# Where the SBUF tiles of a three-layer model kernel begin: tables in front, large tiles on multiples of 256 bytes

## The reference, cut to what matters

```python
q = (hc @ w_query).reshape(PEER_CHUNK, PEER_HEADS, PEER_KEY_DIM)
# top 16 of 128 keys for each half, top 16 of their 256 sums: experts, gate
u = jnp.take(expert_u, experts, axis=0)
act = jax.nn.gelu(jnp.einsum('chkd,cd->chk', u, hc))
v = jnp.take(expert_v, experts, axis=0)
return jnp.einsum('chk,chkd->cd', gate * act, v)
```

## Time and profile before

| | us |
|---|---|
| median of three runs | 3251.67 |
| the profiled execution | 3249.77 |
| its span, first to last instruction | 3247.7 |
| PE busy | 3108.9 |
| POOL busy | 1771.1 |
| DVE busy | 1605.6 |
| ACT busy | 1151.8 |

### The profile page before, as it was taken

One profiled execution on the slowest core, in us unless ns is written; L12 is line 12 of the kernel. 1 busy time (PEld: TensorE's weight loads), 2 busy tenths in 40 slices (PEclk: granted clock), 3 DMA queues, 4 the chain that ended last, 5 costly groups with the idle time before them and its releaser, 6 DMA issues.

```text
span 3247.7 us, 44125 instructions
## 1 busy us (share of the span) xinstructions
PE 3108.9 (96%) x14602; PEld 2502.0 (77%) x14602; DVE 1605.6 (49%) x2785; ACT 1151.8 (35%) x1478; POOL 1771.1 (55%) x2040
## 2 busy tenths in 40 slices
PE   5988999999999999997999999999999999999998
PEld 3777788876578887775788888888888788888886
DVE  7873454322435551694407996444411444444443
ACT  4354322236332213433323325555543322232222
POOL 3833677645047766573455665444446665566663
PEclk8989999999999999998999999999999999999999
DMA  7511455423025553221233444555564655555652
GB/s 304 207 36 61 151 186 191 153 71 96 1 78 200 187 187 112 87 88 61 85 98 112 146 136 169 184 184 184 188 240 141 217 200 186 179 169 196 202 191 72
DMA packets 170201, 481.94 MB, mean 148 GB/s; under 512 B 15360, under 2 KB 48896, under 8 KB 168080
## 3 DMA queue, kind: packets, MB, share of 16 engines
q1 hardware_dynamic: 147680, 410.83, 38.8%
q10 hardware_dynamic: 22448, 70.14, 5.6%
HBM read 411.70 MB, written 69.21 MB: 148 GB/s over the span
## 4 chain that ended last, share of the span: by engine, by line
PE 56%; issue 21%; POOL 19%; DVE 2%; ACT 1%; DMA 0%; DVEq 0%; POOLq 0%; SPq 0%; ACTq 0%
PE ps L1623 52%; POOL w_lo L548 19%; PE pa L1623 3%; DVE s_acc L1417 1%; DMA e_g<-expert_act 0%; DVEq L1414 0%; DVE s_pb L1429 0%; DVE s_tmp L1468 0%; DVE mg_lo L1470 0%; ACT mg_hi L918 0%; DVE s_m L1466 0%; DVE x L1122 0%; ACT L614 0%; POOLq L546 0%; POOLq L552 0%
## 5 line engine op out<-in xcount | busy, mean ns | idle before, releaser
L548 POOL TENSOR_TENSOR w_lo<-raw,w_hi 128x256 fp32r<-128x256 f32 x2036 | 1770.9, 902 | 1446.4 <-ACT w_hi L566 1444.5
L1623 PE MATMUL ps<-h_hi,w_hi 128*128 128x512 f32 x2392 | 950.2, 397 | 43.2 <-POOL w_lo L548 19.6
L1623 PE MATMUL ps<-h_hi,w_lo 128*128 128x512 f32 x2392 | 939.7, 393 | 0.0
L1623 PE MATMUL ps<-h_lo,w_hi 128*128 128x512 f32 x2392 | 915.7, 390 | 0.0
L566 ACT ACTIVATE w_hi<-raw 128x1024 fp32r<-128x1024 f32 x509 | 538.8, 1060 | 844.4 <-PE ps L1623 727.9
L1623 PEld LDWEIGHTS ps<-h_hi,w_hi 128*128 128x128 f32 x2392 | 454.9, 190 | 145.2 <-issue 25.9
L1623 PEld LDWEIGHTS ps<-h_hi,w_lo 128*128 128x128 f32 x2392 | 454.6, 190 | 95.3
L1623 PEld LDWEIGHTS ps<-h_lo,w_hi 128*128 128x128 f32 x2392 | 450.3, 188 | 93.3 <-issue 1.7
L1623 PE MATMUL ps<-wa_hi,w_lo 128*128 128x512 f32 x1024 | 408.6, 399 | 0.0
L1623 PE MATMUL ps<-wa_lo,w_hi 128*128 128x512 f32 x1024 | 403.5, 394 | 0.0
L1623 PE MATMUL ps<-wa_hi,w_hi 128*128 128x512 f32 x1024 | 401.5, 392 | 0.3 <-DVE x L1587 0.3
(11 more groups left out here) (315 smaller groups left out, 3088.7 us busy)
## 6 DMA issues: line engine op xcount, KB each, us to landing
ada<-in_ada SPq DMA_DIRECT2D x144, 512.0 KB, 4.4
raw<-in_expert_u SPq DMA_DIRECT2D x128, 512.0 KB, 4.1
raw<-in_expert_v SPq DMA_DIRECT2D x128, 512.0 KB, 4.2
raw<-in_ffn_in SPq DMA_DIRECT2D x88, 512.0 KB, 3.5
expert_act<-g_act ACTq DMA_DIRECT2D x128, 256.0 KB, 4.3
gate_matrix<-w_st ACTq DMA_DIRECT2D x16, 2048.0 KB, 6.7
e_w<-gate_matrix SPq DMA_DIRECT2D x16, 2048.0 KB, 11.2
e_g<-expert_act SPq DMA_DIRECT2D x128, 256.0 KB, 7.8
```

The lines of the kernel that those rows point to most:

```text
L548: last = nc.gpsimd.tensor_tensor(w_lo[:, k, c:c + 256], raw[:, k, c:c + 256], w_hi[:, k, c:c + 256].bitcast(F32), ALU.subtract)
L1623: return nc.tensor.matmul(out, a, b, start=start, stop=stop_)
```

## The change

The small tables move to the front, behind them `big` is rounded up so that `base + big` is a multiple of 256, and all large tiles, rstd, ada, cvec, keys and the arena follow in their old order at that phase (ada4's 16 bytes now lie in front, AR is no longer rounded). `mg_hi` and `mg_lo`, which were placed at h's old offsets by number, follow `h_off`. `r_z` leaves the arena's end, which is 32 bytes shorter, for the unused part of rstd. No instruction, wait or DMA is added or removed.

```diff
@@ -161,13 +161,7 @@
     K = 1024
-    x = at("x", 0, [DT, S])
-    h_hi = at("h_hi", 16 * K, [DT, S], F32R)
-    h_lo = at("h_lo", 32 * K, [DT, S], F32R)
-    raw = at("raw", 48 * K, [RING, 1024])
-    w_hi = at("w_hi", 64 * K, [RING, 1024], F32R)
-    w_lo = at("w_lo", 80 * K, [RING, 1024], F32R)
-    misc = 96 * K
+    misc = 0
     cols = at("cols", misc, [COLS["end"]])
     misc += 4 * ((COLS["end"] + 7) // 8 * 8)
     mod = at("mod", misc, [144])
@@ -175,6 +169,16 @@
     misc += 768
     consts = at("consts", misc, [CONST["end"]])
     misc += 4 * ((CONST["end"] + 7) // 8 * 8)
+    ada4 = at("ada4", misc, [RING])
+    big = (base + misc + 16 + 255) // 256 * 256 - base
+    x = at("x", big, [DT, S])
+    h_off = big + 16 * K
+    h_hi = at("h_hi", h_off, [DT, S], F32R)
+    h_lo = at("h_lo", big + 32 * K, [DT, S], F32R)
+    raw = at("raw", big + 48 * K, [RING, 1024])
+    w_hi = at("w_hi", big + 64 * K, [RING, 1024], F32R)
+    w_lo = at("w_lo", big + 80 * K, [RING, 1024], F32R)
+    misc = big + 96 * K
     rstd_off = misc
     rstd = at("rstd", misc, [S])
     misc += 2 * K
@@ -187,9 +191,7 @@
     keys = at("keys", misc, [2, NK])
     misc += 1 * K
-    ada4 = at("ada4", misc, [RING])
-    misc += 32
-    AR = (misc + 31) // 32 * 32
+    AR = misc
     arena_bytes = 229344 - base - AR
@@ -267,8 +269,8 @@
-    mg_hi = at("mg_hi", 16 * K, [DT, S], F32R)
-    mg_lo = at("mg_lo", 32 * K, [DT, S], F32R)
+    mg_hi = at("mg_hi", h_off, [DT, S], F32R)
+    mg_lo = at("mg_lo", h_off + 16 * K, [DT, S], F32R)
@@ -292,7 +294,7 @@
-    r_z = ar("r_z", 92 * K, [2, TT, PH])
+    r_z = at("r_z", rstd_off + 64, [2, TT, PH])
```

## The result

The changed kernel took 3228.76 us (median of four, 3223.73 to 3236.50) against 3251.81 for the kernel before (median of four): a ratio of 0.9924 with a 95% interval of 0.9905 to 0.9943. In a second group of runs the same kernel gave 3229.91 against 3249.81, 0.9940 (0.9920 to 0.9961). The change makes the kernel 20 to 23 us faster; 3223 were forecast.

The account below looks back on a forecast made before the run. The prediction took one PE matmul stream to bound nearly everything after 280 us; terms for wa, f, cy, pm and c summed to 29.1 us, taking 3249.77 to 3220.7, or 3223 us as the runs' median. The range was 3205 to 3256.

Parts of the forecast that it names:

- The wa term: Stage streaming wa_hi and wa_lo: 3072 matmuls each 6.6 ns faster, 20.3 us saved.
- The pm and cy terms: Matmuls on pm and cy: 96 each, faster by 5.0 and 6.6 ns, saving 0.5 and 0.6 us.
- c, 0.7: Matmuls on c, 204 with pm's phases: 1.0 us by count, 0.7 taken because the 48 turned ones have less to give.
- The h term: The 7176 matmuls on h, in phase before and after: 0 taken, bounds 97 us gain and 47 us loss.
- The f term: Two FFN output stages streaming f_hi and f_lo: 1056 matmuls each 6.6 ns faster, 7.0 us saved.
- Is it all on the path?: Check in the wa and f stretches that other engines stay under PE's faster pace, POOL next; nothing taken off.
- the sum: All off-phase streams (wa, f, cy, pm, c) going to 226.8 ns a matmul: 29.1 us saved in total.
- The rival of a further gain from a start at 0: A start at 0 speeds the h stream too: 47 us more (3175 us), or 138 on all streams (3084 us); 7%.
- The rival on the other side: The h stream loses its good remainder 128 and pays 6.6 ns a matmul: 47 us added, 3270 us; 6%.
- The rule of 16-byte lines: Skill's SBUF rule: full speed wants two or more hits per 16-byte line; by it alone no stream would gain, sum 0.
- the 111 us on top: Extra gain if alignment alone kept all streams from the skill's 216 ns: 10.8 ns on each of 10248 matmuls.
- the 138 us: Extra gain if all streams reached the 213.3 ns of their columns: 13.5 ns on each of 10248 matmuls, 3084 us.

Follow-up runs that it names:

- e8: Changed kernel with the 12 ada blocks of the FFN output stages issued beside the first 8 weight blocks, not 5: 3224.79 us, ratio to before 0.9921.
- e5: Changed kernel with the weights (raw, w_hi, w_lo) at 192 modulo 256 and everything else at 64, 128 bytes apart: 3280.65 us, ratio to before 1.0088.
- e4: Changed kernel with only the weights (raw, w_hi, w_lo) moved, to 224 modulo 256, the rest at 0: 3284.79 us, ratio to before 1.0098.
- e1: Changed kernel with only the arena 32 bytes later, at 32 modulo 256: 3254.01 us, ratio to before 0.9992.
- e3: Changed kernel with all large tiles and the arena 32 bytes later, all at 32 modulo 256: 3232.22 us, ratio to before 0.9934.
- e7: Changed kernel run again unedited, for its spread and a second profile: 3229.91 us over six runs, ratio to before 0.9940.
- e9: Changed kernel with the weights at 0 modulo 512 and the other large tiles at 256 modulo 512, 256 bytes apart: 3231.24 us, ratio to before 0.9930.
- e6: Changed kernel with the weights (raw, w_hi, w_lo) at 192 modulo 256 and everything else at 0, 64 bytes apart: 3244.39 us, ratio to before 0.9985.
- e2: Changed kernel with only the arena 64 bytes later, at 64 modulo 256: 3231.67 us, ratio to before 0.9937.

## Why the prediction was right

The wa term was 20.3 us: the stage went from 717.55 to 697.50, 20.1 less. The pm and cy terms, 0.5 and 0.6: 22.46 to 21.92 and 22.57 to 21.92, 0.5 and 0.7. c, 0.7: the stage went from 54.56 to 53.94, 0.6. Moving the tables and r_z cost nothing that the traces show, and neither did the new remainder on ACT, DVE and POOL. The h term, taken as 0 between -97 and +47 us, measured 0.0 on the two pieces of the chain; only the longest h stretch (2064 matmuls, router work between them) took 564.82 and 564.81 us in the two profiles, against 563.05 before and 563.69 in e8. What that up to 1.8 us is stays open.

The f term was mis-sized. 7.0 us were forecast; the first profile shows 1.3 + 0.3, the second 2.6 + 2.2, where 3.5 + 4.4 is what the stages give without stops. The step that failed is "Is it all on the path?": it compared the engines' busy times over the middle of an f stage and named POOL as next. What was next is at the stage's start, on SP's queue: ada blocks, each behind a wait for DVE, ahead of weight blocks. The earlier trace rows hides this, since the stretch begins 31 us into the stage; the waits of the stage in the kernel before (us, times, longest) show it:

```profile
ACT w_hi L566 <- DMA raw<-in_ffn_out: 23.2, 3, 12.9
```

The late blocks were there already, and PE at 233 ns was just slow enough to meet them hardly at all (0.9 us in both stages together). The rest of the difference between 29 and 20 to 23 us goes with the clock, as far as the runs show it: beside e5 to e8 the kernel before ranges over 17 us, and in the three groups its runs lose some 2.6 to 3 us for each 0.001 of mean granted clock. Six runs of the changed kernel had a mean of 0.978 beside 0.9805 for the kernel before; two of the first four, at 0.980 and 0.981, took 3223.7 and 3223.9. Whether the short stops of the f stages pull the clock down is not settled: in the first profile it fell to the lower level 1 us after the stop that ends at 1227.91, and e8, which has no such stops, had 0.9797. Over all kernels the mean is 0.981 to 0.982 in e4 and e5, whose streams are all slow, 0.980 in e1 and the kernel before, and 0.978 in e3, e7 and e9. So the clock may give back part of what a faster stream wins; no run separates the two.

The clearest check of the sum is e8's profile beside that of the kernel before, since TensorE was at its lower level about as long in both (127 and 130 us) and neither waits long in an f stage: 3220.04 against 3249.77 us, 29.7 less, where the sum had 29.1 and the edit to the order is worth 0.9 in the old layout. That the changed kernel itself came out within 7 us of 3223 is the mechanism, less what the stops and the clock took; neither of these was a term of the forecast.

The reasoning had the right rule among several, and for this change the number couldn't tell them apart. "Same phase on both sides" and "multiple of 64 or 256" all gave 227 here; e3 separates them, e4 to e6 show the other side, and the title's 256 turned out to be sufficient and not needed. The rival of a further gain from a start at 0 is out with e3 and e9: 227.0 ns is the pace at each common remainder tried (128, 0 and 32). The rival on the other side, that 128 is a good remainder by itself, is out too. Its price of 6.6 ns on the h stream was of the right size: e4 made that stream pay 6.4 ns, and the kernel lost 33 us against before, with a mean granted clock of 0.982 against 0.980. The 10248 matmuls with which the prediction and the expectations price "all streams" are h and wa alone; with all 12084 the 111 us on top would be 131 and the 138 us 163. No chance and no term of the 29.1 us rests on that count.

"TensorE: Matmul & The Clock Gate", Step-by-step: what each phase is for, in the Trainium skill says that PE reads the moving operand and the weights through two independent ports, so that loading the next weights takes nothing from the running matmul. No run here sees the ports, but e4, in which of all remainders only that of the weights is another, makes the same stream 6.4 ns slower; if loading took nothing from the stream wherever the tiles lie, it should have cost nothing. The rule of 16-byte lines in "SBUF — State Buffer", Specifications (TRN2), in the Trainium skill, which the prediction weighed, doesn't tell the kernels apart either: the large tiles of every kernel of this study lie on multiples of 32, and the pace is 227 or 233 ns among them.

## What to carry to other kernels

When a matmul-bound stage runs at a steady pace, divide stretch by count for each pair of operands and compare the paces: a difference of 3% at equal shape and clock came from where the tiles begin. Place streaming and stationary float32r tiles, and both halves of a split one, with the same remainder modulo 256, and check what a table of odd size does to all that lies behind it. Before crediting a faster stream, look at the first microseconds of its stage and at the queue that feeds it, not at the busy shares of its middle.

## What the runs showed of the hardware that was not expected

- The pace of a stream of 128x128 by 512 float32r matmuls depends on the distance of the streaming start from the stationary one modulo 256: 227.0 ns at 0, 229 at 64, 233 at 32, 96, 128, 192 and 224. The remainder itself doesn't count (e3, 32 on both sides, 227).
- Neighbours count: with `pm_hi` at distance 0 and `pm_lo` at 32 or 64 in turn, the matmuls with `pm_hi` took 230 to 232 ns (e1, e2).
- At 64 apart the mean isn't the same everywhere: cy took 233 to 234 ns in e2 and 226 to 232 in e6 at the same distance. In e2 it follows the pm stage with its mixed halves, in e6 one with equal halves; whether that is the cause is open, and so is what owns the 13.7 ns between 227.0 and 512 columns at 2.4 GHz.
- The float32 and bfloat16 matmuls of 128 columns kept 112 and 57 ns in every layout.
- GpSimd's `w_lo` operation took 917 ns in e3 and 919 in e9, and 900 to 906 in all other runs; no remainder explains both.
- Beside e1 to e4 the kernel before took between 3242.74 and 3264.93 us; the runs with the lower mean granted clock are the longer ones.
